# Compressed attention in a decoder layer: gate and rate applied after the value product instead of before the transposes

## What is computed

```
s = jnp.einsum('bqghd,bngd->bghqn', qc, kc).astype(jnp.float32) * scale
dist = (t[:, None] - cmp_end[None, :]).astype(jnp.float32)
valid = cmp_end[None, :] <= t[:, None]
p_cmp = masked_softmax(s - sl * dist, valid) * jnp.any(valid, axis=-1)[:, None].astype(jnp.float32)
o_cmp = jnp.einsum('bghqn,bngd->bqghd', p_cmp.astype(dt), vc)
imp = jnp.einsum('bghqn,nm->bgqm', p_cmp, a_sel)
imp = jnp.where(forced, FORCED_SCORE, imp)
imp = jnp.where(blk_start[None, :] <= t[:, None], imp, -1.0)
_, idx = lax.top_k(imp, k_sel)
...
return gc[..., 0:1] * o_cmp + gc[..., 1:2] * o_sel + gc[..., 2:3] * o_win
```

## Time and profile before

| | us |
|---|---|
| Median of 3 runs (lowest, highest) | 3107.2 (3106.88, 3109.52) |
| Profiled execution, its own time | 3106.81 |
| Its span | 3105.0 |
| The phase of the change, first to last instruction of its engines | 918.9 to 1049.7 of the span |
| PE busy over the whole span | 2792.4 (90%) |
| DVE, ACT, POOL busy over the whole span | 1688.7, 1104.3, 1028.0 |

### The profile page before, as it was taken

The page is one execution under the profiler, slowest core; times in us unless marked ns, Lnnn a source line. Parts: engine busy times, 40 slices in busy tenths (PEclk is TensorE's granted clock), DMA queues, the critical chain, the costliest instruction groups (busy, mean ns, idle before and its releaser), DMA issues. The chain is left out here.

```text
span 3105.0 us, 41130 instructions
## 1 busy us (share of the span) xinstructions
PE 2792.4 (90%) x14110; PEld 1913.3 (62%) x14111; DVE 1688.7 (54%) x3394; ACT 1104.3 (36%) x2274; POOL 1028.0 (33%) x982
## 2 busy tenths in 40 slices
PE   8989999999976799999999899999899999579980
PEld 4668888888864465665545566666444455456760
DVE  6675556655547566666666578887222222422227
ACT  0012222222235355555555456666211122123322
POOL 1266777866613402112130201100222333011116
PEclk9999999999987699999999999999999999689995
DMA  3333234232353101110020111100864244365848
GB/s 130 132 130 109 102 109 165 101 109 102 109 183 147 36 8 59 37 65 11 30 77 20 48 55 42 42 1 1 333 192 115 93 156 137 124 237 203 351 164 316
DMA packets 150215, 355.30 MB, mean 114 GB/s; under 512 B 13840, under 2 KB 61584, under 8 KB 143888
## 3 DMA queue, kind: packets, MB, share of 16 engines
q1 hardware_dynamic: 129776, 278.47, 25.8%
q0 software_dynamic: 13824, 50.34, 4.8%
q10 hardware_dynamic: 6432, 24.12, 2.0%
HBM read 230.52 MB, written 122.36 MB: 114 GB/s over the span
## 5 line engine op out<-in xcount | busy, mean ns | idle before, releaser
L566 ACT ACTIVATE p_kept<-p_a 128x256 f32<-128x256 f32 x336 | 129.0, 384 | 463.6 <-PE p_a L512 463.5
L1536 DVE CUSTOM_DVE_ANT_0 b_prob_s<-b_pq,b_sel 128x640 f32<-128x640 f32 (+5 forms) x192 | 168.6, 911 | 129.8 <-PE b_pq L1428 123.1
L1464 PE MATMUL b_po<-b_probT,vsw 128*64 128x256 f32 (+1 forms) x1824 | 231.7, 372 | 0.0
L1389 POOL TENSOR_TENSOR b_rate<-gates,b_total 128x256 f32<-128x256 f32 x64 | 37.9, 614 | 578.5 <-DVE b_total L1550 578.5
L1831 DVE CUSTOM_DVE_ANT_0 d_prob<-d_pq,d_bias 128x1024 f32<-128x1024 f32 (+6 forms) x192 | 168.1, 910 | 68.6 <-PE d_pq L1723 66.4
L1488 ACT ACTIVATE b_prob_s<-b_prob_s,b_neg 128x1152 f32<-128x1152 f32 (+15 forms) x128 | 152.8, 1196 | 128.2 <-DVE b_neg L1544 128.0
L1428 PE MATMUL b_pq<-ks,b_q 64*128 64x512 f32 (+3 forms) x688 | 165.1, 543 | 17.0 <-DVE b_seg_max L1536 8.6
L1559 DVE COPY b_probT<-b_pt 128x512 f32<-128x512 f32 (+1 forms) x253 | 152.5, 630 | 46.3 <-PE b_pt L1451 46.0
L1723 PE MATMUL d_pq<-d_keys,d_q 64*128 64x512 f32 (+3 forms) x576 | 165.8, 561 | 4.9 <-DVE d_seg_max L1831 3.9
L1451 PE MATMUL b_pt<-ident,b_prob_s 128*128 128x128 f32 x1088 | 158.2, 282 | 7.5 <-DVE b_probT L1559 7.1
L1464 PEld LDWEIGHTS b_po<-b_probT,vsw 128*64 128x64 f32 x1824 | 107.3, 136 | 92.1 <-issue 54.3
(11 more groups left out here) (379 smaller groups left out, 6069.8 us busy)
## 6 DMA issues: line engine op xcount, KB each, us to landing
projT<-p_result SPq DMA_DIRECT2D x64, 512.0 KB, 2.8
y<-e_y ACTq DMA_DIRECT2D x43, 512.0 KB, 4.4
p_w<-in_wt SPq DMA_DIRECT2D x16, 1024.0 KB, 7.1
p_w_more<-in_wt SPq DMA_DIRECT2D x16, 1024.0 KB, 6.2
gates_T<-projT SPq DMA_DIRECT2D x64, 256.0 KB, 4.3
wgu<-in_w_gu SPq DMA_DIRECT2D x4, 4096.0 KB, 14.8
y<-b_q POOLq DMA_DIRECT2D x20, 512.0 KB, 21.2
p_xin<-in_x SPq DMA_DIRECT2D x16, 512.0 KB, 3.9
```

Source lines behind the costliest of these rows:

```text
L1464: mm = nc.tensor.matmul(po[u % 2][g * HD:(g + 1) * HD, o:o + w], s.vsw[:, kb, v0 + g * HD:v0 + (g + 1) * HD], probT[:, f % 4, g * w:(g + 1 ...
L1536: nc.vector.tensor_tensor_reduce(out=to, in0=pq[g][:, 0:nb * P], in1=away, scale=slopes[PAIRS * g + i], scalar=-3e38, op0=ALU.add, op1=ALU ...
```

## The change

The exponentials are transposed as they are. The gate and the rate are applied behind the value product, where a factor per token stands along the columns, so it has to be laid out as a matrix first.

- The value matrix `vc` gets 32 more columns per group, the overlap matrix. One product of 96 rows then gives the 64 value rows and the 32 importance rows (`values`, now 96 x 512 for each group, and a PSUM bank `a_po` for each group).
- GpSimd writes, for each step, `a_weights`: 64 columns of gate times rate and 32 columns of the rate, for 8 tiles (`make_weights`). TensorE transposes these into the same banks `a_po` (`spread_weights`), ScalarE copies one bank and VectorE the other to `a_factor` (`keep_factor`), TensorE then writes the product over them, and VectorE multiplies the product with the factor as it evicts (`evict`).
- GpSimd adds up the 32 importance rows over a chunk (`a_seen`), and TensorE transposes the sum into the same bank (`turn_sum`), from which VectorE takes it for the choices.
- The row sums come from the exponentials' accumulator instead of a reduction on VectorE.
- SyncE's loads for the next phase are put between the stores; a step has two stores of 64 rows. GpSimd's mask additions stand ahead of its last `add_up`.
- The buffers `gated`, `plain`, `pbar` and `sumT`, and GpSimd's memsets of them, go.

On GpSimd:

```
+            def make_weights(n):
+                c, i = steps[n]
+                rate = stat[:, n % 4, 3].rearrange("p g t -> p t g")
+                by = s.gates[:, 4 * c:4 * c + 4, :].rearrange("p t (g i b) -> p b i t g", g=GROUPS, b=3)[:, 0, i]
+                pool.wait_ge(rate_ready, n + 1)
...
+                if n >= 2:
+                    pool.wait_ge(spread, n - 1)
+                    pool.wait_ge(summed, n - 1)
+                nc.gpsimd.tensor_tensor(weights[:, n % 2, :, :, 0:HD], by.unsqueeze(3).to_broadcast([P, 4, GROUPS, HD]),
+                                        rate.unsqueeze(3).to_broadcast([P, 4, GROUPS, HD]), ALU.mult).then_inc(weight_ready, 1)
+                nc.gpsimd.tensor_copy(weights[:, n % 2, :, :, HD:ROWS], rate.unsqueeze(3).to_broadcast([P, 4, GROUPS, NBLK])).then_inc(weight_ready, 1)
             def add_up(n):
                 c, i = steps[n]
+                acc, new = seen[HD:ROWS, c % 2], y[HD:ROWS, n % 2]
+                pool.wait_ge(evicted, n + 1)
+                pool.wait_ge(weight_ready, 2 * min(n + 2, NS))
...
+                    nc.gpsimd.tensor_copy(acc, new).then_inc(summed, 1)
                 else:
                     pool.wait_ge(summed, n)
+                    nc.gpsimd.tensor_tensor(acc, acc, new, ALU.add).then_inc(summed, 1)
+            make_weights(0)
             for n in range(NS):
+                if n + 1 < NS:
+                    make_weights(n + 1)
+                if n == NS - 1:
...
+                            mask_row(s, nc.gpsimd.tensor_tensor, 0, j, g).then_inc(s.b_first_masked, 1)
                 add_up(n)
```

On TensorE, whose loop over n now ends with `turn_sum`, where a chunk is full, and `spread_weights(n)`:

```
+            def spread_weights(n):
+                pe.wait_ge(weight_ready, 2 * n + 2)
                 if n >= 1:
                     pe.wait_ge(evicted, n)
...
+                        mm = nc.tensor.transpose(po[g][0:ROWS, j * P:(j + 1) * P], weights[:, n % 2, j, g, :], s.ident[:])
+                mm.then_inc(spread, 1)
+            def values(n):
+                w = width(n)
+                pe.wait_ge(copied, n + 1)
+                pe.wait_ge(factor_ready, GROUPS * (n + 1))
...
+                    mm = nc.tensor.matmul(po[g][0:ROWS, :], s.vc[0:w, g, :], probT[0:w, n % 2, g, :], start=True, stop=True)
                 mm.then_inc(valued, 1)
+            def turn_sum(c):
+                pe.wait_ge(summed, PAIRS * (c + 1))
+                pe.wait_ge(evicted, min(PAIRS * (c + 1) + 1, NS))
...
+                        mm = nc.tensor.transpose(pi[:, g, j, :], seen[HD:ROWS, c % 2, g, j * P:(j + 1) * P], s.ident[HD:ROWS, HD:ROWS])
```

On ScalarE:

```
-                        op = nc.scalar.activation(x, x, ACT.Exp, bias=stat[:, n % 4, 1, g, j:j + 1], scale=slopes[PAIRS * g + i])
+                        op = nc.scalar.activation(x, x, ACT.Exp, bias=stat[:, n % 4, 1, g, j:j + 1], scale=slopes[PAIRS * g + i],
+                                                  accum_out=stat[:, n % 4, 2, g, j:j + 1])
...
+                copy(n)
                 if n + 2 < NS:
                     exponentials(n + 2)
+                keep_factor(n)
```

On VectorE:

```
+            def evict(n):
+                dve.wait_ge(valued, n + 1)
+                dve.wait_ge(factor_ready, GROUPS * (n + 1))
                 if n >= 2:
+                    dve.wait_ge(stored[n % 2], 32 * (n // 2))
+                    dve.wait_ge(summed, n - 1)
+                for g in range(GROUPS):
+                    op = nc.vector.tensor_tensor(y[0:ROWS, n % 2, g, :], po[g][0:ROWS, :], factor[0:ROWS, g, :], ALU.mult)
+                op.then_inc(evicted, 1)
...
                 if n < NS:
+                    rates(n)
                 if n + 2 < NS:
                     maxima(n + 2)
+                if 1 <= n <= NS:
+                    evict(n - 1)
                 if n in sel_choice:
                     choose(*sel_choice[n])
+                if n < NS:
+                    keep_factor(n)
```

More of the change, by code:

```diff
@@ L860, in compressed_attention @@
     NS = len(steps)
-    LAST = NS + 5
+    LAST = NS + 3
     slopes = [2.0 ** (-8.0 * (h + 1) / N_ALIBI) for h in range(NSA_HEADS)]
[L863 to L872, removed]
+    sel_turn = {PAIRS * c + PAIRS + 1: c for c in range(NCH)}
+    sel_choice = {PAIRS * c + PAIRS + 1 + g: (c, g) for c in range(NCH) for g in range(GROUPS)}
+    ROWS = HD + NBLK
     with ExitStack() as ctx:
@@ L875, in compressed_attention @@
         prob = [sb(f"prob{k}", [P, GROUPS, 4, P]) for k in range(4)]
-        gated = [sb(f"gated{k}", [P, GROUPS, 4, P]) for k in range(2)]
-        plain = sb("plain", [P, GROUPS, 4, P])
-        pbar = [sb(f"pbar{k}", [P, GROUPS, 4, P]) for k in range(2)]
         probT = sb("probT", [P, 2, GROUPS, 512])
-        sumT = sb("sumT", [P, GROUPS, 512])
-        y = sb("y", [P, 2, 512])
+        weights = sb("weights", [P, 2, 4, GROUPS, ROWS])
+        factor = sb("factor", [P, GROUPS, 512])
+        y = sb("y", [P, 2, GROUPS, 512])
+        seen = sb("seen", [P, 2, GROUPS, 512])
         imp = sb("imp", [P, GROUPS, 4, NBLK])
@@ L997, in _ @@
                 if n < NS:
[L998 to L999 removed]
+                    turn(n)
                 if 1 <= n <= NS:
@@ L1045, in _ @@
             exponentials(1)
-            for n in range(LAST):
-                if n < NS:
-                    copy(probT[:, n % 2], step_use[n], values_at[n - 2] if n >= 2 else 0)
-                if 1 <= n <= NS:
-                    evict(n - 1)
-                if n in sel_turn:
-                    c = sel_turn[n]
-                    copy(sumT, sum_use[c], weights_at[c - 1] if c >= 1 else 0)
+            for n in range(NS):
+                copy(n)
                 if n + 2 < NS:
                     exponentials(n + 2)
+                keep_factor(n)
         @block.vector
@@ L1082, in maxima, with rates @@
                                                in1=s.cmp_slope[:, i], op0=ALU.max, op1=ALU.mult).then_inc(neg_ready, 1)
-            def gate(n):
+            def rates(n):
                 c, i = steps[n]
-                w = width(n)
-                x = prob[n % 4][:, :, :, 0:w]
-                total, rate, weight = (stat[:, n % 4, k] for k in (2, 3, 4))
-                by = s.gates[:, 4 * c:4 * c + 4, :].rearrange("p t (g i b) -> p b i g t", g=GROUPS, b=3)[:, 0, i]
+                total, rate = (stat[:, n % 4, k] for k in (2, 3))
                 dve.wait_ge(exp_done, n + 1)
-                link(nc.vector.tensor_reduce(total, x, AX.X, ALU.add))
                 if c == 0:
```

156 lines of the change are left out of this document (68 added, 88 removed).

## The result

The changed kernel takes 3138.4 us (3133.9 to 3142.2, 4 runs), the kernel before beside it 3108.4: a ratio of 1.0101, 95% interval 1.0088 to 1.0115. It is slower, as forecast, but by 30 us and not by 7, and outside the range. The profiled execution took 3133.9 us with a span of 3132.1, 27.1 more than the span before.

What follows compares the result with a forecast made beforehand. No engine filled the old phase; a chain between engines bound it, and a one-bank loop would decide the new one. 18.7 + 89.6 + 4.8 + 20.5 + 4.3 = 137.9 us against 130.8, giving 3114 us, range 3099 to 3135.

Steps and rivals of the forecast that it cites:

- The stall of 14.0 goes: ScalarE's wait to rewrite its output buffer, its store queued behind eight large loads, counted as gone: -14.0 us.
- Start, 18.7: From the phase's start at 918.9 to the end of the first eviction, at low clock: 18.7 us.
- The loop, 6.4 high and 10.7 low: Scores, transposes, product, eviction, weights' transposes through one bank, per step: 6.4 us at high clock, 10.7 at low.
- Choices, 1.6 each: Choices of chunks 0 to 2, between eviction and the weights' transposes: 1.6 us each, 4.8 in all.
- Tail, 20.5: Behind step 14's eviction: GpSimd's sum, masks and last sum, then the turning and two choices: 20.5 us.
- I count one loop of 14: 4.3: Spells of low clock among the 14 loops: one loop at low clock, costing 4.3 us more.
- 137.9: The whole phase with all terms summed: 137.9 us against 130.8, 7.1 us more.
- the clock stays low half of the loops: Rival: half of the loops at 1.2 GHz, 30 us in place of 4.3, 3140; chance 0.15 for six loops or more.
- The forecast without its low loop: The phase's forecast sum without the 4.3 us counted for one loop at low clock: 133.6 us.
- I see no effect: Next phase: same data, start behind the same barrier, so no change in time expected there.

Runs made afterwards that it cites:

- order-of-loads run: The kernel before, with SyncE's loads for later phases issued between the stores and no longer ahead of all of them: 3094.0 us, 0.9959.
- the narrow filler: The changed kernel with one more matmul per loop, 32 rows by 32 columns, ahead of the weights' transposes, its result never read: 3137.9 us, 1.0104.
- the run with the product's rows: The changed kernel with only the value product using all 128 rows in every chunk, turns and copies kept narrow: 3117.9 us, 1.0036.
- Own banks: The changed kernel with 128 product rows, and the weights' transposes written to the turned exponentials' banks, not the product's: 3117.4 us, 1.0038.
- halved stores: The kernel before, with each of the compressed branch's 16 stores made in two of 64 rows: 3105.4 us, 1.0000.
- the number of stores: The changed kernel with 128 product rows, weights' transposes in other banks and masks spread, its two stores per product made one DMA: 3111.2 us, 1.0017.
- the run with the loads first: The changed kernel with all loads ahead of the first store again: 3141.7 us, 1.0109.
- 128-row filler: The changed kernel with one more matmul per loop, 128 rows by 128 columns, ahead of the weights' transposes, its result never read: 3117.6 us, 1.0028.

## Why the prediction was wrong, step by step

- *The stall of 14.0 goes*: right, by the trace of the changed kernel and by the order-of-loads run. What it was worth was more, as the low clock behind it goes too: the phase without the stall was put at 116.8 us, and that run's lasted 111.8.
- *Start, 18.7*: 18.4 measured (916.9 to 935.3, the end of the first eviction).
- *The loop, 6.4 high and 10.7 low*: right, 6.3 to 6.5 and 10.8, the same in chunk 1 and chunk 3. TensorE idles 1.4 to 1.5 us per loop for the eviction, and 1.97 in one. The product takes 1.88 to 1.96 (1.8 counted): two with 96 rows of output do not run side by side.
- *Choices, 1.6 each*: right within what the rows tell. The nine loops from 986.73 to 1046.93 hold those of two chunks and take 60.2; 9 x 6.4 + 2 x 1.6 = 60.8.
- *Tail, 20.5*: 19.1 (1048.2 to 1067.3). The 32-row sum takes 2.34 and not 3.22, twice 0.9 less.
- **The step that failed: "I count one loop of 14: 4.3" of low clock.** The five loops from 933.97 to 986.73 took 52.8 us, where five at the high clock with one chunk's choices would have taken 5 x 6.4 + 1.6 = 33.6. So this term was 19.2: 14.9 more than counted, against 12.5 by which the phase missed its 137.9. The rest, -2.4, is the start, the tail and the nine loops.

The term was mis-sized because it was drawn from TensorE's busy share (4.80 of 5 us at clock 1.00, 4.04 of 5 at 0.81). The share does not decide it in these runs. The products of before had 128 rows in every chunk, zeros among them; the change cut them to 32, 64 and 96, and the clock stayed low while they had 32. That is in the diff, and the prediction had no term for the rows: it took the product's time from rows of 128. With 128 rows the changed kernel is 20 to 22 us faster, and its phase lasts 133.8 us (916.7 to 1050.5) in place of 150.4. The rival "the clock stays low half of the loops" was nearest in time (3140), but by luck. It had the low clock cost 30 us, where it cost 19.2, and nothing behind the phase, where 9.5 came. Its mechanism was another too: it named the share of transposes, and the narrow filler lowered that share with the clock still at 0.50. The Trainium skill's rule on transposes (TensorE: Matmul & The Clock Gate, Part 4: PE-mode transpose), cited in the prediction, does not tell the runs apart either: the run with the product's rows has the transposes of the changed kernel, and its clock is 0.89 from 935 to 967 where that one's is 0.50.

What is left then is 10 us over the kernel before. By the trace only 3 of them lie in the phase (133.8 us against 130.8), 5 at the merge. The forecast without its low loop was 133.6, so the stall that goes and the dearer loop nearly cancel, as it had them; the run still has one slower loop (7.9 us from 939.18 to 947.06). Against the kernel before with the new order of loads (111.8 us) the phase is 22 us too long: 14 in the 14 loops (97.2 against 82.9), 6 in the tail (19.1 against 13.5) and 2 at the start. A loop takes 6.3 us in every chunk, where that kernel takes 4.0 between its evictions at 939.1 and 947.2. Own banks did not lift this, as they moved the wait to the copies.

*Wrong too: "I see no effect" on later phases.* From the start of the phase ahead of the merge to that of the merge, the kernel before takes 15.7 us. All twelve versions built on the changed kernel, itself among them, take 4.5 to 5.6 us more, with one yaT_spill issue of 7.7 to 8.7 us; none of the five built on the kernel before takes more than 0.8 more (issues of 2.8 to 3.5). Not its cause: the order of loads, halved stores, the number of stores, the clock in chunks 0 and 1. What it is stays open. The 3 us or so behind it stay open too; they differ from run to run (the run with the loads first lost none there).

## What to carry to other kernels

Cutting the product to the rows in use saved no time by itself here, and with 32 rows it cost TensorE's clock in two kernels. So before counting a high clock, look at how many rows the products of that stretch have, not only at how busy TensorE is, and measure. The zero rows that were already there were worth 16.6 us of the phase in the changed kernel and 8.4 in the other, by the traces. A change of several parts is to be priced part by part: here the two that touch no new wait (order of loads, accumulators) bring 26 us, and the rest takes back more than that, even with 128 rows in its products (3117.9 against 3082.9). And the wait that was removed by moving a tile to another bank came back as a wait for the copies that free that bank.

## What the runs showed of the hardware

- TensorE busy for 15.00 of 15 us at a granted clock of 0.50, with products of 32 rows between turns of 128 by 128; 1.00 with products of 128 rows and TensorE busy for 12.17. Where a 128-row filler stood beside them, products of 32 rows ran at the high clock (1.95 us in place of 3.73).
- A VectorE addition of two inputs in SBUF, 128 columns, took 0.28 us with GpSimd idle and 2.43 beside the masks. One that has a single input was held back too: in the changed kernel the operation that writes the block mask (`sel_mask`) took 1.00 to 1.01 us beside GpSimd's sum and 0.23 without.
- GpSimd's addition of 1024 elements took 2.34 us on 32 partitions and 3.22 on 128: the time follows the length of a row, but not alone.
